# Query, key and value projections as a Strassen stage of their own, gate projections among the attention units

## The reference

```
h = RMSNorm(x)
qa, ka, va, qb, kb, vb, gates = split(h @ w_in)       # 3*512 + 512 + 2*128 + 2*1024 columns
y_a = chunked attention (8 heads, own chunk + 8 before, learned bias) @ w_branch_a
y_b = sliding-window attention (8 query, 2 key heads, rotary, sinks) @ w_branch_b
x = x + (sigmoid(gate_a) * y_a + sigmoid(gate_b) * y_b) @ w_out
h2 = RMSNorm(x);  x = x + (silu(g) * u) @ w_down      # g, u = halves of h2 @ w_gate_up
```

## Time and profile before

| | us |
|---|---|
| median of 3 runs | 2823.6 (2822.61 to 2824.02) |
| the profiled execution | 2826.14 |
| its span, first to last instruction | 2824.4 |
| PE busy | 2752.5 (97%) |
| DVE busy | 1828.5 (65%) |
| ACT busy | 1120.1 (40%) |
| POOL busy | 355.9 (13%) |
| idle of PE before a high-by-high matmul on h | 17.5 |

### The profile page before, as it was taken

The page is one execution under the profiler, slowest core; times in us unless marked ns, Lnnn a source line. Parts: engine busy times, 40 slices in busy tenths (PEclk is TensorE's granted clock), DMA queues, the critical chain, the costliest instruction groups (busy, mean ns, idle before and its releaser), DMA issues.

```text
span 2824.4 us, 38044 instructions
## 1 busy us (share of the span) xinstructions
PE 2752.5 (97%) x13528; PEld 2305.4 (82%) x13528; DVE 1828.5 (65%) x3790; ACT 1120.1 (40%) x2307; POOL 355.9 (13%) x206
## 2 busy tenths in 40 slices
PE   7899999999999999999989999999999999999998
PEld 6788888888878888888868888888888788888887
DVE  5566664225688778767865666642356887877687
ACT  4665652002343333344545666520024333333444
POOL 3111112333200000000021111132331000000000
PEclk9999999999999999999999999999999999999998
DMA  5101001113222223376330101011131233323943
GB/s 198 31 24 39 32 23 39 45 52 112 104 86 97 94 101 109 112 236 177 103 128 32 32 24 39 16 50 47 45 134 75 97 105 112 112 98 111 276 127 120
DMA packets 132260, 253.56 MB, mean 90 GB/s; under 512 B 10752, under 2 KB 56064, under 8 KB 131328
## 3 DMA queue, kind: packets, MB, share of 16 engines
q1 hardware_dynamic: 124064, 215.02, 23.4%
q10 hardware_dynamic: 8032, 36.40, 3.5%
HBM read 190.03 MB, written 61.34 MB: 89 GB/s over the span
## 4 chain that ended last, share of the span: by engine, by line
PE 91%; DVE 5%; ACT 2%; issue 1%; DMA 0%; ACTq 0%; DVEq 0%
PE ps L622 14%; PE ps L624 14%; PE ps L623 14%; PE ps L610 13%; PE ps L615 12%; PE ps L614 12%; PE ps L758 5%; PE ps L743 3%; PE ps L728 1%; PE ps L729 1%; ACT swapped L1048 1%; DVE sumsq L1421 1%; PE ps L769 1%; DVE rope L1494 0%; DMA up_raw<-w_gu 0%
## 5 line engine op out<-in xcount | busy, mean ns | idle before, releaser
L622 PE MATMUL ps<-op_hi,up_hi 128*128 128x512 f32 x1232 | 482.5, 392 | 11.1 <-issue 4.9
L623 PE MATMUL ps<-op_lo,up_hi 128*128 128x512 f32 x1232 | 481.5, 391 | 0.0
L624 PE MATMUL ps<-op_hi,up_lo 128*128 128x512 f32 x1232 | 481.1, 390 | 0.0
L610 PE MATMUL ps<-h_hi,w_hi 128*128 128x512 f32 x1088 | 449.4, 413 | 17.5 <-DVE h_lo L1405 16.9
L615 PE MATMUL ps<-h_hi,w_lo 128*128 128x512 f32 x1088 | 429.2, 394 | 0.0
L614 PE MATMUL ps<-h_lo,w_hi 128*128 128x512 f32 x1088 | 428.5, 394 | 0.0
L592 POOL CAST w_hi<-w_raw 128x1024 fp32r<-128x1024 f32 x100 | 105.1, 1051 | 1781.4 <-PE ps L610 1120.7
L622 PEld LDWEIGHTS ps<-op_hi,up_hi 128*128 128x128 f32 x1232 | 232.3, 189 | 62.7 <-issue 7.8
L1199 ACT ACTIVATE up_hi<-up_raw 128x512 fp32r<-128x512 f32 x264 | 165.0, 630 | 294.3 <-PE ps L624 274.2
L624 PEld LDWEIGHTS ps<-op_hi,up_lo 128*128 128x128 f32 x1232 | 232.6, 189 | 48.7
L623 PEld LDWEIGHTS ps<-op_lo,up_hi 128*128 128x128 f32 x1232 | 232.4, 189 | 48.0
(11 more groups left out here) (174 smaller groups left out, 4739.7 us busy)
## 6 DMA issues: line engine op xcount, KB each, us to landing
w_raw<-w_lin SPq DMA_DIRECT2D x100, 512.0 KB, 3.2
up_raw<-w_gu SPq DMA_DIRECT2D x44, 1024.0 KB, 5.0
act_raw<-ff_saved SPq DMA_DIRECT2D x154, 256.0 KB, 2.7
ff_saved<-ff_block SPq DMA_DIRECT2D x88, 256.0 KB, 2.0
ff_saved<-ff_mix SPq DMA_DIRECT2D x66, 256.0 KB, 2.0
dn<-w_dn_a SPq DMA_DIRECT2D x48, 256.0 KB, 4.1
dn<-w_dn_b SPq DMA_DIRECT2D x40, 256.0 KB, 3.7
x_saved<-x_sb ACTq DMA_DIRECT2D x2, 4096.0 KB, 12.7
```

The costliest lines, as they stand in the source:

```text
L610: mm = pe.matmul(out, w_hi[slot][:, k, :], hi, start=first, stop=False)
L622: pe.matmul(out, w1, x1, start=first, stop=False, skip_group_check=True)
L623: pe.matmul(out, w1, x0, start=False, stop=False, skip_group_check=True)
L624: return pe.matmul(out, w0, x1, start=False, stop=last, skip_group_check=True)
```

## The change

- The projections of query, key and value become a stage of their own ahead of attention, by Strassen's scheme as in stage 5: 9 pairs of tiles, seven products each (`project`). Its seven operands are sums of the quarters of gain times x (`turn_sum`, `third_sum_in`, `fourth_sum_in`, `raise_in_op`, `lower_in_op`), its weights are mixed and split by ACT and DVE (`mix_in`, `split_in`), no longer by POOL. The results are scaled by `rstd` and written to DRAM (`in_saved`).
- Attention reads them back by halves, in the order `CONV`, at the units `CONV_START`, into two `stage` buffers (`load_half`). The swapped rows of a rotary half are read by four DMAs of 32 rows, no longer copied by ACT.
- The steps between the units are gate steps, 28 of the 32 halves (`fill_steps`): one step a unit in A phases, 2 or 3 in B phases. Each half is scaled into a `logit` buffer and written to DRAM (`gates_saved`). The last four halves follow attention (`last_gates`), in two parts.
- The branch projections then run with no gates between them; the gates are loaded for each tile and half (`load_gates`) and opened by ACT. The mixed result goes to operands of its own (`m_hi`, `m_lo`) at once.
- The first layer loads x by quarters. In the second layer a part of the operand making runs inside the first layer's Down stage (`lead_in`), in place of `take_new`.
- x is read back in one DMA. The loops over tiles on TensorE, POOL, SP, DVE are written out.

```diff
+IN_FIRST = (0, 1, 3, 4, 2, 5, 6)
+IN_ORDER = tuple((q, i) for i in IN_FIRST for q in range(2)) + tuple((q, i) for q in range(2, IN_PAIRS) for i in range(PRODUCTS))
+CONV_START = (-2, -1, 0, 1, 3, 5, 6, 8, 10, 12, 14, 15) + tuple(
+    g * UNITS_PER_GROUP - PHASE + r for g in range(1, GROUPS) for r in (2, 4, 6, 8, 10, 12, PHASE + 2, PHASE + 6))
...
+            def load_half(L, c):                              # SP
+                kind, g, half = CONV[c]
...
+                    sp.wait_ge(done, L * each + rank(c - 2) + 1)
+                sp.wait_ge(in_kept[2 * (t % 2) + 1 - half], in_kept_at(L, t // 2))
+                sp.dma_start(stage[c % 2][:, :], in_dram[t, half]).then_inc(stage_loaded[c % 2], 16)
+                if CONV_CLASS[kind] == "rope":
+                    if rank(c) == 0:
+                        sp.wait_ge(in_done, (L + 1) * IN_STEPS)
+                    else:
+                        sp.wait_ge(rope_sum, L * ROPES + rank(c))
+                    for quad in range(4):
+                        other = quad ^ 1
+                        sp.dma_start(swapped[32 * quad:32 * quad + 32, :], in_dram[t, half, 32 * other:32 * other + 32, :]) \
+                          .then_inc(swap_loaded, 16)
...
+            def project_all(L):                               # TensorE
+                for s, (q, i) in enumerate(IN_ORDER):
+                    project(L, q, i)
+                    if s == 7:
+                        sum_columns(2 * L)
+                    if s == 8:
+                        spread_rstd(2 * L)
...
             def attention(L):
-                for k in range(KT + LAG):
...
+                for k in range(FILL_FIRST):
+                    gate_step(L, *divmod(k, KT))
+                pe.wait_ge(in_taken, in_takes(L, IN_PAIRS - 1, 6))
                 for s in range(UNITS + 4):
...
+                    for c in conv_at(s, "va", "vb"):
+                        turn_values(L, c)
...
+                project_all(L)
                 attention(L)
...
+                last_gates(L)
+                for n in range(KT):
+                    branches(L, n)
...
+            def lead_in(L, st):                               # DVE, inside down
+                if 38 <= st < 42:
+                    add_square_in(L, st - 38)
+                if 60 <= st < 64:
+                    lower_in_op(L, 0, st - 60)
+                if 63 <= st < 67:
+                    add_square_in(L, XK + st - 63)
+                if st in (69, 70):
+                    mix_in(L, st - 69, 0)
+                    mix_in(L, st - 69, 1)
+                if st in (70, 71):
+                    split_in(L, st - 70, 0)
+                if 71 <= st < 75:
+                    turn_sum(L, st - 71)
+                if 73 <= st < 77:
+                    lower_in_op(L, 1, st - 73)
+                if st == 75:
+                    third_sum_in(L, 0)
+                    third_sum_in(L, 1)
+                    split_in(L, 0, 1)
+                if st == 76:
+                    third_sum_in(L, 2)
+                    third_sum_in(L, 3)
+                    split_in(L, 1, 1)
+                    for k in range(XK):
+                        lower_in_op(L, 3, k)
+                    for j in range(2 * XK, 3 * XK):
+                        add_square_in(L, j)
...
+            def start_in(L):                                  # DVE
+                if L == 0:
+                    for k in range(XK):
+                        lower_in_op(0, 0, k)
...
+                for k in range(XK):
+                    fourth_sum_in(L, k)
...
+                for k in range(XK):
+                    lower_in_op(L, 2, k)
+                take_in(L, 1, 3)
+                for j in range(3 * XK if L > 0 else XK, IN_SUMS):
+                    add_square_in(L, j)
+                split_in(L, 0, 2)
+                split_in(L, 1, 2)
...
+                take_in(L, 0, 4)
+                for k in range(XK):
+                    lower_in_op(L, 5, k)
+                take_in(L, 1, 4)
+                split_in(L, 0, 5)
+                split_in(L, 1, 5)
+                split_in(L, 0, 6)
+                split_in(L, 1, 6)
+                for k in range(XK):
+                    lower_in_op(L, 6, k)
+                norm(2 * L)
...
+            def turn_half(L, c):                              # DVE
...
+                dve.wait_ge(stage_loaded[c % 2], 16 * (L * (len(CONV) // 2) + c // 2 + 1))
+                dve.tensor_tensor(stage[c % 2][:, :], stage[c % 2][:, :], rope[:, 0, tokens(half)], ALU.mult).then_inc(rope_step, 1)
+                dve.wait_ge(swap_loaded, 64 * (L * ROPES + n + 1))
+                dve.tensor_tensor(swapped[:, :], swapped[:, :], rope[:, 1, tokens(half)], ALU.mult).then_inc(rope_step, 1)
```

More of the change, by code:

```diff
@@ L44 @@
 FIRST_PIECE = 2 * P
-LAG = 4
 NPROBS = 3
@@ new lines, in _ @@
+                load(L, GATE_TILES)
+                for half in range(NHALF):
+                    load_gates(L, 0, half)
+                load(L, GATE_TILES + 1)
+                for i in range(FILL_HALVES, GATE_HALVES):
+                    keep_logit(L, i)
+                load(L, GATE_TILES + 2)
+                for n in range(1, KT):
+                    for half in range(NHALF):
+                        load_gates(L, n, half)
+                    load(L, GATE_TILES + 2 + n)
+                for n in range(2, KT):
+                    load(L, TILES - KT + n)
@@ L626, in sum_columns @@
             def sum_columns(n):
[L628 removed]
+                pe.wait_ge(sum_ready, sq_base(n + 1) + 1)
+                out, src = (bank(5), sumsq) if n % 2 else (bank(1), rstd)
+                if n % 2 == 0:
+                    pe.wait_ge(x_new, 4 * n + 8)
                 for b in range(NBLK):
[L630 removed]
+                    mm = pe.matmul(out[:, b:b + 1], src[:, b * P:(b + 1) * P], ones[:, :], start=True, stop=True)
                 mm.then_inc(col_done, 1)
@@ new lines, in add_square_in @@
+            def add_square_in(L, j):
+                _, half = sq_quarter(L, j)
+                first = all(sq_quarter(L, other)[1] != half for other in range(j))
+                dst = rstd[:, tokens(half)]
+                dve.wait_ge(sq_ready, sq_base(2 * L) + j + 1)
+                if first:
+                    if L > 0:
+                        dve.wait_ge(up_scaled, 3 * L * FF_TILES)
+                    dve.tensor_copy(dst, sq_buffer(L, j)[:, :]).then_inc(sum_ready, 1)
+                else:
+                    dve.wait_ge(sum_ready, sq_added(L, j - 1))
+                    dve.tensor_tensor(dst, dst, sq_buffer(L, j)[:, :], ALU.add).then_inc(sum_ready, 1)
@@ L1972, in down @@
                     else:
-                        i, odd = divmod(st - 6 * PAIRS - 4, 2)
-                        if 0 <= i < XK and not odd:
-                            take_new(L, i)
+                        lead_in(L + 1, st)
                 if L == DEPTH - 1:
```

1264 lines of the change are left out of this document (834 added, 430 removed).

## The result

The changed kernel takes 2895.75 us (median of 4 runs, 2893.91 to 2905.99) against 2823.8: ratio 1.0262, 95% interval 1.0238 to 1.0287. It is 72 us slower; forecast was 2797, 27 us faster. The profiled execution took 2893.91, of which its span is 2892.1.

What follows compares the result with a forecast made beforehand. TensorE's large matmuls, 0.227 us each, were taken as the bound. Terms -49.0 + 20.0 + 9.1 - 10.8 + 0 + 4.5 = -26.2 take 2826.1 to 2799.9, median 2797 us; range for 8 in 10: 2774 to 2817.

Steps and rivals of the forecast that it cites:

- 1. Products removed: Query, key and value projections: 108 large matmuls fewer a layer, 216 in all, at 0.227 us each: -49.0 us.
- 2 and 3. The starts: Projection starts wait for DVE's rstd: +20.0 us in layer 0 (12 to 30), +9.1 in layer 1 with Down (3 to 18).
- step 6: Clock: after the waits in the new projection starts TensorE runs some matmuls at half pace: +4.5 us (0 to 8).
- 1 us for it (0 to 6): Layer 0's Down: cost of the added DVE operations that prepare layer 1's projections.
- the ring of four steps: Layer 0's Down, steps 69 to 75: said to take most of the 4.6 us by which DVE's work exceeds TensorE's.
- 4. Attention: Only phase 0 moves, its stall falling from 13.4 to 8 us: -5.4 a layer, -10.8 in all; stall range 2 to 20.
- By it up to 3 us a layer more: Attention: cost of DVE operations with two SBUF inputs and POOL excluding each other, said to lie within the stall's range.
- 5. Gates and branches: Last gate halves and branch projections: same work, an 8 us gate chain hidden under 10.9 us of branches: 0 (-3 to +8).
- The end of +8: Gates and branches, upper end: +8 us if the 4 MB read of x slows the gate loads.
- C: Rival: slower, conversions bound every attention group as SP, ACT and DVE wait for DMAs: +60, 2857 us; chance 0.07.
- The 0.87 for faster: Whole kernel: chance given to a time faster than 2818 us, that is by more than 0.2%.
- the "-3" of step 5: Gates and branches, lower end: -3 us, since 3.5 were lost there before the change.

Runs made afterwards that it cites:

- r10_rate: r7_mend plus a reordered projection start, with two gate steps a unit instead of one in attention's phase 0 and fewer in later B phases: 2807.4 us, ratio 0.9938.
- r11_tuned: r10_rate with the rotary halves' conversions spaced so that a turn, a low part and a gate scaling avoid sharing a unit step: 2806.1 us, ratio 0.9937.
- r12_down: The changed kernel with layer 1's preparation in steps 69 to 75 of layer 0's Down moved behind its last step: 2897.5 us, ratio 1.0257.
- r5_late: The changed kernel with rotary query halves of head groups 1 to 3 converted six unit steps later, swapped-row loads placed apart: 2870.5 us, ratio 1.0162.
- r3_norot: The changed kernel without the three DVE operations that turn a rotary half, DMAs and their waits kept: 2853.4 us, ratio 1.0104.
- r1_act: The changed kernel with ACT raising both halves of a mixed tile before opening the next tile's gates: 2873.0 us, ratio 1.0174.
- r2_sp: The changed kernel with SP issuing the last four gate halves' DRAM writes ahead of the second branch tile's load: 2895.4 us, ratio 1.0253.
- r6_xback: The changed kernel with x read back in eight 512 KB DMAs inside the branch loop instead of one of 4 MB: 2888.1 us, ratio 1.0224.
- r7_mend: The changed kernel with ACT's branch order changed, x read back in parts, POOL's low parts in four pieces and later rotary query halves: 2833.3 us, ratio 1.0035.

## Why the prediction was wrong, step by step

**1. Products removed.** Right: 216 matmuls fewer, Up's spacing as before, and where nothing else binds, the saving appears (r10_rate and r11_tuned are faster than the kernel before). One reading was wrong without harm: Up has 24 DVE operations a pair (535 in 22 pairs), not "31 DVE operations a pair and more"; 24 is still more than the 20 of the new stage.

**2 and 3. The starts.** The mechanism was right, DVE's queue with `rstd` behind the ninth product: DVE delivered rstd at 70.3, forecast 65.8, and TensorE went on with the products at 73.8, forecast 67.8. Of the 4.5 us on DVE, 2.56 are a wait for x from DRAM, which the step had called "in time". The stage ended 7.6 late in the profiled execution, 3.6 at the least in the others. Part of it is the clock (0.92 in the stage), for which step 6 had 2.2 a layer. In layer 1, 3.8 over, though the two waits came as forecast: 4.1 us before the second product (3.7) and 5.8 for rstd (5.3). "1 us for it (0 to 6)" for Down was mis-sized: +7.2, outside its range. The excess of 4.6 us of DVE over TensorE that the step worked out was nearly the answer; "mostly taken by the ring of four steps" threw it away, and r12_down gives it back: 3.6.

**4. Attention, the step that failed.** Forecast -5.4 a layer, measured 28 and 31 more than that. Phase 0, the only place where it looked for a change, gave 1.1 of the 5.4 in layer 0 and nothing in layer 1; the rest of the miss is in the groups behind it. It said that in later groups "a rotary half is loaded well ahead". That was true: in all of layer 0's attention units DVE waited for the swapped rows once, for 0.2 us, for the staged halves not at all, and TensorE once, 1.9 us at the start of phase 0 (the waits of DVE in the changed kernel, 222.8 to 596.4):

```profile
DVE swapped L2146 <- DMA swapped<-in_saved: 0.2, 1, 0.2
```

But it answered only whether the data are there, not where the three operations on them stand. The kernel before had one of a group's two rotary query halves in the A phase, 20 us into it, in its long units; the other stood in the B phase behind it, beside three steps a unit (timeline of DVE of the kernel before, phases 2 and 3):

```profile
200.22 0.69 DVE L1445 SCALAR_TENSOR_TENSOR turning<-ps,rope 128x512 f32<-128x512 f32 x1 [0.22 <-ACT swapped L1048]
...
225.20 0.68 DVE L1445 SCALAR_TENSOR_TENSOR turning<-ps,rope 128x512 f32<-128x512 f32 x1
```

The change puts both into the A phases, with one step a unit, at units 2 and 6, and a gate scaling in the same unit. The windows of a phase could not tell: TensorE was busy for 37.36 of phase 2's 37.8 us, and still r5_late puts all of this work into it and takes 37.8. "No other engine comes forward" was argued from phase 7, a B phase with two steps a unit; the sum of DVE's work was compared, its places were not. r3_norot (those operations out: -20 a layer), r5_late (same operations, later: -13 and -11) and r10_rate (more cover in phase 0: -9 and -7) agree on it. "By it up to 3 us a layer more" for DVE and POOL excluding each other was too small: splitting POOL's instruction alone made the units 7.9 and 9.7 us shorter and the attention stage 4.7 and 6.5. Most of that lies in the B phases, where 38 steps now cover what 48 did; what the low parts and what the 128x1 operation cost there is not taken apart. The 1.22 against 2.83 us of the same operation shows that the exclusion lasts one instruction of POOL. The Trainium skill (SBUF - State Buffer, Who interferes with whom) has the rule that the prediction named, and these rows agree with it; what the prediction missed is that the length of the other engine's single instruction is the price, and can be chosen.

**5. Gates and branches, the second failure.** Forecast 0 with ends -3 and +8, measured +16 and +13. "m of n-1 done, load (...), two sigmoids, about 8 us, hidden under 10.9 us of branches" counted the chain of one half. There are two halves a tile, and ACT's written order makes one wait for the other's load: 2 x 6.24 = 12.5. r1_act removes it with no work removed: -9 a layer. The end of +8 named x's 4 MB read, but slowing the gate loads; it slows the logit writes ahead of them (r2_sp; r6_xback: -7 and -4). With both cured the stage takes 86.8 us in r7_mend, which is the 0 of the forecast.

**6. Clock.** +4.5 was for the starts alone. The 59 us more at the lower level came with the stalls and went with them: in r11_tuned the clock is back at 0.990.

**The rivals.** C had the sign and, at 2857, came nearest, with 0.07, but by its number alone. Its mechanism, SP, ACT and DVE waiting for DMAs in every group, is refuted by the waits above; its price, work of the conversions showing on TensorE, was the right kind. The 0.87 for faster rested on each stage's sums of work against TensorE's, and those sums held: r11_tuned does the same matmuls, the same DVE and ACT operations, and takes 2806.

What is not taken apart: the excesses named add up to 7.6 + 3.8 + 28.1 + 31.3 + 15.6 + 13.1 + 6.2 - 4.5 = 101.2, 7 more than the miss of 94. 3.5 of these are what the kernel before lost around layer 0's gates and branches, the "-3" of step 5, gone with the change; the rest is spread over stages that each differ by about 1.

## What to carry to other kernels

Before you call an operation hidden, find the unit of the schedule in which it will stand, and set it against what the bottleneck engine has to do in that unit. A busy share does not answer this: the same phase, 99% busy, took a burst for nothing in its long units and lost 6 us to it in its short ones. Where one engine's instruction can hold up another engine's, even a tiny operation in the chain can wait for the whole of it; keep such instructions short. In a loop over halves with in-order engines, follow the free-load-use circle of one buffer through every engine's written order, and multiply by the number of halves. Issue big transfers in parts where small ones that someone waits for are still to come.

## What the runs showed of the hardware

- Two DVE operands in SBUF against POOL: a multiplication of 128x512 took 2.83 us beside a POOL subtraction of 128x1024 (2.84), 1.22 beside the same in four pieces, and 0.69 alone. Four pieces cost POOL 4.17 instead of 2.84 there; the mean over the 64 tiles is 3.6 instead of 2.54.
- A tiny DVE operation waits as well: an addition of 128x1, 0.16 us as a rule, took 2.15 beside the POOL subtraction (2.38) and 0.50 beside the pieces.
- A 256 KB write issued 0.6 us behind another queue's 4 MB read landed after some 14 us instead of 2.2.
- DVE work of 20.7 us a layer, in bursts of 2.1 between two row maxima, cost TensorE 20 us. With the six query halves of the later groups moved by six units and the four halves of phase 0 left in place, 7 and 8 us of that stayed, over half of it in phase 0.
